# A stick-breaking suffix sum as two single-pass products, and one level of a gated recurrence over four row groups

## The reference, cut to what matters

```python
z = einsum('bhtd,bhsd->bhts', q, k) * scale
log_fail = where(strict, log_sigmoid(-z), 0.0)
log_after = cumsum(log_fail, axis=3, reverse=True) - log_fail
w = where(strict, exp(log_sigmoid(z) + log_after), 0.0)
out = einsum('bhts,bhsd->bhtd', w, v)
```

```python
diff = b[:, :, :, None, :] - b[:, :, None, :, :]        # b: cumulated log forget gates
decay = exp(minimum(diff, 0.0)) * tri[:, :, None]
A = einsum('bhtsd,bhsd->bhts', q[:, :, :, None, :] * decay, k)
o = einsum('bhts,bhsv->bhtv', A, v) + (what comes from the state before the chunk)
```

## Time and profile before

| | us |
|---|---|
| median of 3 runs | 996.64 |
| lowest, highest | 995.03, 997.21 |
| the profiled execution | 997.04 |
| its span, first to last instruction | 995.2 |
| mean granted clock of TensorE in it | 0.996 |

### The profile page before, as it was taken

The page is one execution under the profiler, slowest core; times in us unless marked ns, Lnnn a source line. Parts: engine busy times, 40 slices in busy tenths (PEclk is TensorE's granted clock), DMA queues, the critical chain, the costliest instruction groups (busy, mean ns, idle before and its releaser), DMA issues.

```text
span 995.2 us, 18822 instructions
## 1 busy us (share of the span) xinstructions
PE 983.3 (99%) x8050; PEld 890.0 (89%) x8050; DVE 672.6 (68%) x896; ACT 593.6 (60%) x829; POOL 25.4 (3%) x26
## 2 busy tenths in 40 slices
PE   8999999999999999999999999999999999999996
PEld 7899987888989999998899999889899999987985
DVE  5675688867755788875556565785695556588565
ACT  7677576574537656654446676537754765654581
POOL 0000000000000000000000003000000000130000
PEclk9999999999999999999999999999999999999999
DMA  8762434656565665557654553553556446534331
GB/s 297 270 200 92 150 115 161 210 170 205 176 193 191 187 192 171 170 169 253 190 156 148 147 173 115 163 158 129 172 168 193 151 118 190 170 129 142 137 128 42
DMA packets 97283, 166.45 MB, mean 167 GB/s; under 512 B 6896, under 2 KB 32240, under 8 KB 96816
## 3 DMA queue, kind: packets, MB, share of 16 engines
q1 hardware_dynamic: 95792, 159.18, 50.7%
q0 software_dynamic: 976, 4.46, 1.3%
q10 hardware_dynamic: 432, 1.62, 0.4%
HBM read 164.19 MB, written 1.05 MB: 166 GB/s over the span
## 4 chain that ended last, share of the span: by engine, by line
PE 94%; DVE 2%; ACT 2%; issue 1%; DMA 1%; SPq 0%; DVEq 0%; ACTq 0%
PE proj L623 14%; PE proj L624 14%; PE proj L625 14%; PE proj L632 13%; PE proj L634 13%; PE proj L633 13%; PE mix L668 1%; PE mix L944 1%; PE mix L693 1%; PE mix L676 1%; PE mix L905 1%; PE mix L893 1%; DMA raw<-in_w_mem_kv 1%; ACT arena L1372 1%; PE mix L701 1%
## 5 line engine op out<-in xcount | busy, mean ns | idle before, releaser
L1532 DVE TENSOR_TENSOR wlo<-raw,whi 128x1024 fp32r<-128x1024 f32 (+2 forms) x304 | 356.6, 1202 | 177.3 <-ACT whi L1067 176.0
L1067 ACT ACTIVATE whi<-raw 128x1024 fp32r<-128x1024 f32 (+2 forms) x304 | 307.3, 1040 | 185.4 <-PE proj L634 81.3
L623 PE MATMUL proj<-act_hi,whi 128*128 128x256 f32 x1064 | 304.0, 286 | 0.5 <-ACT arena L1345 0.5
L624 PE MATMUL proj<-act_lo,whi 128*128 128x256 f32 x1064 | 301.0, 283 | 0.0
L625 PE MATMUL proj<-act_hi,wlo 128*128 128x256 f32 x1064 | 301.0, 283 | 0.0
L623 PEld LDWEIGHTS proj<-act_hi,whi 128*128 128x128 f32 x1064 | 203.2, 191 | 3.0 <-ACT arena L1345 1.4
L624 PEld LDWEIGHTS proj<-act_lo,whi 128*128 128x128 f32 x1064 | 203.3, 191 | 0.5
L625 PEld LDWEIGHTS proj<-act_hi,wlo 128*128 128x128 f32 x1064 | 203.2, 191 | 0.2
L632 PE MATMUL proj<-whi,y_hi 128*128 128x512 f32 (+1 forms) x340 | 133.3, 392 | 1.3 <-DVE wlo L1532 1.3
L634 PE MATMUL proj<-whi,y_lo 128*128 128x512 f32 (+1 forms) x340 | 132.3, 389 | 0.0
L633 PE MATMUL proj<-wlo,y_hi 128*128 128x512 f32 (+1 forms) x340 | 132.3, 389 | 0.0
(11 more groups left out here) (335 smaller groups left out, 1027.4 us busy)
## 6 DMA issues: line engine op xcount, KB each, us to landing
raw<-in_w_in SPq DMA_DIRECT2D x144, 512.0 KB, 4.4
raw<-in_w_up SPq DMA_DIRECT2D x88, 256.0 KB, 4.4
raw<-in_w_out SPq DMA_DIRECT2D x32, 512.0 KB, 3.5
raw<-in_w_down SPq DMA_DIRECT2D x22, 512.0 KB, 5.7
raw<-in_w_mem_k SPq DMA_DIRECT2D x8, 512.0 KB, 4.0
raw<-in_w_o SPq DMA_DIRECT2D x8, 512.0 KB, 3.9
raw<-in_w_mem_v SPq DMA_DIRECT2D x8, 512.0 KB, 4.1
raw<-in_w_mem_kv SPq DMA_DIRECT2D x7, 512.0 KB, 6.7
```

What stands on the lines that cost most here:

```text
L623: mm(o, wh[:, i, wc], hi[:, k0 + i, :], start=begin and j % 2 == 0, stop=False, skip_group_check=True)
L624: mm(o, wh[:, i, wc], lo[:, k0 + i, :], start=False, stop=False, skip_group_check=True)
L1067: fn(whi[c % SPLIT][:, 0:w], raw[c % SLOTS][:, 0:w], ACT.Copy).then_inc(s.w_hi, 1)
L1532: tt(wlo[c % SPLIT][:, 0:w], raw[c % SLOTS][:, 0:w], f32(whi[c % SPLIT][:, 0:w]), ALU.subtract).then_inc(s.w_lo, 1)
```

## The change

The logarithms are split as weights are: ScalarE rounds them into `SB_hi`, VectorE takes the remainder into `SB_lo` (in parts of `y_hi` and `y_lo` that are free then), and TensorE multiplies both by rounded constants, which are exact (ones and eights). The two products by `suffix` on one head become one of 384 columns. ScalarE and VectorE do three of their splits before these new steps, the rest of them after. In the level of half 64, the two token blocks go to different row groups of one bank instead of the same row groups in two banks, and `leave_64` copies by token block.

```diff
--- before.py
+++ after.py
@@ -241,6 +241,8 @@
         self.sb_a = new("sb_a")
         self.sb_l = new("sb_l")
         self.sb_m = new("sb_m")
+        self.sb_mh = new("sb_mh")
+        self.sb_ml = new("sb_ml")
         self.sb_c = new("sb_c")
         self.sb_e = new("sb_e")
         self.sb_x = new("sb_x")
@@ -379,6 +381,7 @@
         arena = sb("arena", [P, 16384])
         total = sb("total", [P, 2016])
         ones_r = sb("ones_r", [P, P], F32R)
+        sums_r = sb("sums_r", [P, 2 * P], F32R)
 
         proj = [ctx.enter_context(nc.psum_tensor(f"proj{i}", [P, NB, 512], F32)) for i in range(2)]
         mix = ctx.enter_context(nc.psum_tensor("mix", [P, 4, 512], F32))
@@ -502,6 +505,7 @@
                  16: total[:, 1792:1920], 32: total[:, 1920:1984], 64: total[:, 1984:2016]}
         HQT, HSQ, HV, HGT = ar(14336, 8, SEQ), ar(10240, 8, SEQ), ar(12288, NB, DM), ar(8192, 8, SEQ)
         LNG, LNB = ar(12288, DM), ar(13312, DM)
+        SB_hi, SB_lo = (v[:, 12:18, :].rearrange("p k t -> p (k t)").rearrange("p (h t) -> p h t", t=TRI) for v in (y_hi, y_lo))
         C_hi, C_lo = y_hi[:, 8:11, :], y_lo[:, 8:11, :]
         MEM_hi, MEM_lo = y_hi[:, 14:22, :], y_lo[:, 14:22, :]
         def sides(half, four):
@@ -750,12 +754,13 @@
                 last.then_inc(s.sb_z, 1)
                 project(more[0], None, act_hi, act_lo, part=(1, 4))
                 project(more[1], None, act_hi, act_lo, part=(0, 1))
-                pe.wait_ge(s.sb_m, grp + 1)
-                for hh in range(4):
-
-                    mm(mix[:, hh, 0:SEQ], cst("suffix"), SBB[:, hh, 0:SEQ], start=False, stop=False, skip_group_check=True)
-                    mm(mix[:, hh, P:SEQ], cst("eights"), SBB[:, hh, SEQ:TRI], start=False, stop=False, skip_group_check=True)
-                    last = mm(mix[:, hh, SEQ:TRI], cst("suffix"), SBB[:, hh, SEQ:TRI], start=False, stop=True, skip_group_check=True)
+                pe.wait_ge(s.sb_mh, grp + 1)
+                for part, side in enumerate((SB_hi, SB_lo)):
+                    if part:
+                        pe.wait_ge(s.sb_ml, grp + 1)
+                    for hh in range(4):
+                        mm(mix[:, hh, 0:TRI], sums_r[:, 0:P], side[:, hh, :], start=False, stop=False, skip_group_check=True)
+                        last = mm(mix[:, hh, P:SEQ], sums_r[:, P:2 * P], side[:, hh, SEQ:TRI], start=False, stop=part == 1, skip_group_check=True)
                 last.then_inc(s.sb_c, 1)
                 project(more[1], None, act_hi, act_lo, part=(1, 4))
                 pe.wait_ge(s.sb_w, grp + 1)
@@ -931,7 +936,6 @@
                             pe.wait_ge(s.hg_cp, 6 * L + 4)
                         elif l == 1:
                             pe.wait_ge(s.mla_g, 2 * L + 2)
-                            pe.wait_ge(s.hg_cp, 6 * L + 6)
                         elif l == 0:
                             pe.wait_ge(s.hg_cp, 6 * L + 5)
                             pe.wait_ge(s.hg_ca, 6 * L + 2)
@@ -950,8 +954,8 @@
                             elif l == 1:
                                 for b in range(NB):
                                     for j in range(2):
-                                        t, at_col = b * P + 32 * j, 128 * (h % 4) + 64 * b
-                                        last = mm(mix[32 * j:32 * j + 32, four, at_col:at_col + 64], zk[:, t:t + 32], zq[:, b * P + 64:b * P + P], start=True, stop=True)
+                                        t, row, at_col = b * P + 32 * j, 64 * b + 32 * j, 64 * h
+                                        last = mm(mix[row:row + 32, 0, at_col:at_col + 64], zk[:, t:t + 32], zq[:, b * P + 64:b * P + P], start=True, stop=True)
                             else:
                                 for j in range(4):
                                     at_col = P * (h % 4)
@@ -1212,6 +1216,9 @@
                 act.wait_ge(s.sb_a, grp + 1)
                 link(fn(SBA, SBA, ACT.Exp, scale=-1.0))
                 fn(SBA, SBA, ACT.Ln, bias=1.0).then_inc(s.sb_l, 1)
+                split_until(ahead_of("mlv" if grp else "mlq", None, 2))
+                act.wait_ge(s.sb_m, grp + 1)
+                fn(SB_hi, SBB, ACT.Copy).then_inc(s.sb_mh, 1)
                 if grp == 0:
                     leave("mlq", None, PRE[:, 0:4, :])
                 else:
@@ -1401,10 +1408,10 @@
 
                 def leave_64():
 
-                    for four in range(2):
-                        act.wait_ge(s.hg_pr, 18 * L + 15 + four)
-                        src = mix[0:64, four, :].rearrange("p (h b t) -> p h b t", h=4, b=NB)
-                        fn(both(AT[0:64, 4 * four:4 * four + 4, 64:P], 4, 64), src, ACT.Copy).then_inc(s.hg_ca, 1)
+                    act.wait_ge(s.hg_pr, 18 * L + 16)
+                    for b in range(NB):
+                        src = mix[64 * b:64 * b + 64, 0, :].rearrange("p (h t) -> p h t", h=HG_H)
+                        fn(AT[0:64, :, b * SEQ + 64:b * SEQ + P], src, ACT.Copy).then_inc(s.hg_ca, 1)
 
                 def leave_128():
 
@@ -1637,6 +1644,7 @@
             tt(LBX[:, 8:16], logits[:, 1, :], logits[:, 0, :], ALU.subtract).then_inc(s.lb_a, 1)
             copy(cur[:, 0:1], cols3[:, 2:3])
             copy(ones_r[:, :], ones)
+            copy(sums_r[:, :], const[:, CONST_AT["suffix"][0]:CONST_AT["eights"][1]])
             copy(cur[:, 1:3], cols3[:, 4:6])
             copy(cur[:, 3:4], cols3[:, 8:9])
             dve.wait_ge(s.rows_in, 32)
@@ -1682,6 +1690,9 @@
                 dve.wait_ge(s.sb_l, grp + 1)
                 link(tt(SBB, SBB, SBA, ALU.subtract))
                 tt(SBB, SBB, over(cst("strict"), 4), ALU.mult).then_inc(s.sb_m, 1)
+                split_until(ahead_of(more[0], None, 2))
+                dve.wait_ge(s.sb_mh, grp + 1)
+                tt(SB_lo, SBB, f32(SB_hi), ALU.subtract).then_inc(s.sb_ml, 1)
                 split_until(pieces_until(more[0], None))
                 dve.wait_ge(s.sb_c, grp + 1)
                 ts(SBB, z, 0.0, None, ALU.min).then_inc(s.sb_e, 1)
```

## The result

The changed kernel takes 1001.03 us (median of 6 runs, 998.46 to 1001.81) where the kernel before took 996.63 in the same comparison: 1.0046 of it, 95% interval 1.0034 to 1.0058. It is slower by 4.4 us, outside the forecast range. The profiled execution took 1001.43, its span is 999.6, 4.4 above the span of before.

The account below looks back on a forecast made before the run. TensorE, busy 99% of the span, was taken to bound the kernel. Suffix stages +1.9 us and the level of 64 -1.55 us summed to +0.35, 997.0 us on the median; bounds 996.6 to 998.8, 8-in-10 range 995.0 to 999.0.

Parts of the forecast that it names:

- What bounds the kernel: Whole kernel: TensorE is busy 99% of the span, so a microsecond in its queue is a microsecond of the kernel.
- The wait on the lower side: Suffix stages: TensorE waits 2.1 and 2.6 us for VectorE's subtraction behind three splits; the stages lose 0.65 and 1.25 us.
- The straight line for the rounded products: Suffix products: a line through rounded 256 and 512 columns gives 0.24 us a head for 384 plus 128, 0.96 a side.
- the dear products: Rival, 12%: rounded suffix products cost their upper bound, 0.45 us a head; the stages cost 3.6 and the kernel takes 998.7.
- The level of 64: products(1) over four row groups instead of two takes 1.14 us instead of 1.91, saving 0.77 per layer, 1.55 in two.
- The clock: Rival, 5%: TensorE's clock falls in the new suffix waits, some 1.9 us a fall, two 3.8; kernel 999 to 1001.
- granted clock at 1.00 behind both waits: Sign expected in the new profile: TensorE's clock stays at full level after both suffix-stage waits on the subtraction.
- What was unseen: The 2% chance left for something that neither the forecast nor its rivals named.
- Removed: per head one product of 256 columns and two of 128, in two passes each: Suffix stages: the old products taken out, counted as time of 0.43, 0.22 and 0.22 us per head.

Follow-up runs that it names:

- after_again: The changed kernel with no edit, run again for a second profile: 1000.40 us (6 runs), ratio 1.0041 to the kernel before.
- level_only: The kernel before with the change of the level of 64 alone, suffix sums as before: 993.95 us (11 runs), ratio 0.9977.
- early_three: early_lower with each side's 384 columns done as 256 and 128, bringing TensorE back to 8050 passes: 993.10 us (11 runs), ratio 0.9976 to the kernel before.
- suffix_only: The kernel before with the change of the suffix sums alone, level of 64 as before: 1001.77 us (6 runs), ratio 1.0051.
- early_lower: The changed kernel with one VectorE split before the subtraction and two behind it: 994.51 us (12 runs), ratio 0.9991 to the kernel before.
- mid_lower: The changed kernel with two VectorE splits before the subtraction instead of three: 995.69 us (11 runs), ratio 1.0000 to the kernel before.
- no_eights: The kernel before without the eight products by the constant of eights, 8034 passes instead of 8050: 996.14 us (11 runs), ratio 1.0009.

## Why the prediction was wrong

*What bounds the kernel*: right. Each wait and each gain of TensorE showed in the end time.

*The wait on the lower side*: right in mechanism and place. The subtraction starts behind the third split and ends at 108.35, 0.25 after the forecast and as late as this execution started (0.27), and at 140.59, where the forecast 138.06 and the 2.60 that it ran late by then make 140.66. TensorE waited 1.78 and 2.19 us (forecast 2.1 and 2.6). The second stage lost 1.43 (forecast 1.25). The first lost 1.35, of which some 0.5 is the low clock at its end: its last two heads take 0.53 each instead of 0.29. That leaves 0.85 (forecast 0.65).

*The straight line for the rounded products* failed by a little. A pair of 384 and 128 columns takes 0.29 to 0.30 of TensorE's queue (105.59 to 105.89), not 0.24. How that divides is not shown: from the 384 to its 128 it is 0.23 in most pairs and 0.18 in the first (105.36 to 105.54). This is 0.2 to 0.25 a side, inside the bounds (up to 0.45 a head); the wait hides it on the upper side, on the lower one nothing does. So the dear products were right in part of their price and not the cause.

*The level of 64*: right, 0.72 and 0.82 where 0.77 was forecast. The floor of some 25 ns that the Trainium skill gives ("TensorE: Matmul & The Clock Gate", "Wait — 56ns, not 53.3ns?") would have left 1.6 of the level; 64 passes took 1.19, 18.6 ns each, and the measurement decides.

*The clock* was the rival with 5%, and it came to pass: all three profiles with these waits have a fall at one of the two, and by the mean clocks most runs have one; "granted clock at 1.00 behind both waits" is the line of the prediction that failed. The evidence against it came from the end of the kernel, where TensorE was idle with the clock still at 1.00 for some time; the waits here were no longer, and I read that as safe. The nearer row was overlooked: the clock of the kernel before itself fell at 179 us, behind 2 us of thin products. Its price was right: a fall costs 1.5 in the profile of the changed kernel (0.5 in the stage and 0.98 behind it, against 1.9), and more in after_again, where it stayed low longer.

*What was unseen*, with 2% left for it: the step "Removed: per head one product of 256 columns and two of 128, in two passes each" counted the passes as time and nothing else. Taking 16 of them out also moved every later instruction, and TensorE then waits 1.8 to 2.9 us behind `products(8)` of the second layer. All five profiled kernels with 8034 passes have it at that place (the changed one twice), none of the three with 8050 has it. With the fall that can follow, it is 2 to 4.7 us; the 0.44 us of waiting at 917 us that goes away in exchange are some 0.7 in its favour.

In sum: 2.1 to 2.3 for the two stages at full clock, near 1.5 to 3 for falls behind them, 2 and more for the wait on issue, and 1.5 given back by the level (in the profiled executions also the fall at 179 us, 1.6, that only the one of before had), against 4.4 measured. How the falls share out over the unprofiled runs can't be told one by one; their mean clocks (0.993 to 0.996, one of 0.998) say that most had one or two more than the kernel before (0.996 to 0.998).

*What the wait on issue is.* The DMA queue for instructions (q8) moves 1.03 MB in 63 packets in either kernel, 16 KB each; that comes to some 64 bytes for each of TensorE's 16,068 or 16,100 passes and weight loads, so by size it is TensorE's stream. The traces hold the start of every packet. The 52nd of the 63 stands in these windows, 880.0 to 883.8 us of the kernel before (ahead of `products(8)`) and 888.0 to 890.4 of the changed kernel (inside its wait; packets, MB, share of 16 engines):

```profile
q8 instruction: 1, 0.02, 2.3%
q8 instruction: 1, 0.02, 2.5%
```

| profile | passes | `products(8)` starts | 52nd packet starts | TensorE goes on after its wait |
|---|---|---|---|---|
| before | 8050 | 883.87 | 880.31 | no wait |
| level_only | 8050 | 881.09 | 877.15 | no wait |
| early_three | 8050 | 880.57 | 877.12 | no wait |
| the changed kernel | 8034 | 885.28 | 888.10 | 890.46 |
| after_again | 8034 | 887.03 | 888.83 | 891.11 |
| suffix_only | 8034 | 886.23 | 888.29 | 890.73 |
| early_lower | 8034 | 879.87 | 881.80 | 883.98 |
| mid_lower | 8034 | 881.55 | 883.43 | 885.85 |
| no_eights | 8034 | 881.63 | 883.55 | 885.74 |

With 8050 passes this packet starts 3.45 to 3.94 us ahead of `products(8)`, with 8034 it starts 1.80 to 2.82 us behind the start of `products(8)`, and there TensorE goes on 2.2 to 2.4 us after the packet's start, every time, however long it has waited. So the wait is, by its times, one for a late packet of instructions. No record names the packet as what released TensorE, and why 16 passes move its start by over 5 us against `products(8)` stays open. That the place in the stream decides is shown, from both sides.

## What to carry to other kernels

When an operand is split into an upper and a lower part by other engines, the second part's place in their queues decides, not the products: here moving one subtraction ahead of two weight splits turned a loss into a small gain. A wait of some 2 us on an otherwise full TensorE should be priced with a chance of a fall of the clock (1.5 us and more here): in the profiles, 5 of the 12 waits of 1.8 to 2.9 us had one, and none of those up to 1.1 us at the suffix stages. An edit that changes the number of TensorE's instructions can shift a stall to or from a place that it never touched, so before a loss is put down to an edit's logic, the same edit with the old count is worth a run.

## What the runs showed that was not expected

A wait on issue of 1.8 to 2.9 us came and went with 16 passes of 8050, 750 us before it, and ended each time 2.2 to 2.4 us after a packet of the instruction queue started. The granted clock fell at one of the two waits of 1.8 and 2.2 us in each of three profiles, and at none of the suffix waits up to 1.1 us in the profiles of early_lower and mid_lower; once low, it stayed so for 3 us in one profile and over 6 in another. In the kernel before it fell with no wait at all, behind 2 us of products on 4 partitions. A rounded pair of 384 and 128 columns takes 0.29 to 0.30 us of TensorE's queue, not the 0.24 of a line through 256 and 512.
